# Down projection of a gated FFN as seven 128-token block products per 256 outputs, with a one-pass gate activation and VectorE's loop written out

## What is computed

```python
def conv_glu_ffn(h, w_up, conv_w, conv_b, w_down):
    u = causal_depthwise_conv(h @ w_up, conv_w) + conv_b
    gate, up = jnp.split(u, 2, axis=-1)
    return (jax.nn.gelu(gate, approximate=True) * up) @ w_down
...
        x = x + rms_norm(conv_glu_ffn(h, w_up[l], ffn_conv_w[l], ffn_conv_b[l], w_down[l]), ffn_post_norm[l])
```

## Time and profile before

| what | us |
|---|---|
| median of three runs | 1795.56 |
| lowest and highest of them | 1792.64, 1796.88 |
| span of the profiled execution, first to last instruction | 1791.1 |
| TensorE busy | 1704.2 |
| VectorE busy | 642.6 |
| ScalarE busy | 409.8 |

### The profile page before, as it was taken

How to read it: one execution, slowest core, us unless ns; L and a number is a source line. 1 busy time by engine, 2 the same in 40 slices (tenths; PEclk the granted TensorE clock), 3 DMA queues, 4 the chain that set the end, 5 groups by cost and what they waited for, 6 DMA issues and landing times.

```text
span 1791.1 us, 20952 instructions
## 1 busy us (share of the span) xinstructions
PE 1704.2 (95%) x8474; PEld 977.6 (55%) x8474; DVE 642.6 (36%) x1289; ACT 409.8 (23%) x797; POOL 32.2 (2%) x58
## 2 busy tenths in 40 slices
PE   9999999999999999999899999989899889988897
PEld 8778788887888888888623222322222222222232
DVE  3574466612759999941211101111010101111001
ACT  1143122201263544530111111111110111111112
POOL 4000000000000000100000000000000000000000
PEclk9999999999999999999999999999999999899999
DMA  5340244433453434276799999999999999999998
GB/s 187 118 188 13 83 157 148 163 148 116 166 191 118 168 133 169 104 291 249 304 374 433 433 425 436 430 430 433 431 430 430 430 431 435 430 432 428 432 432 335
DMA packets 36389, 523.07 MB, mean 292 GB/s; under 512 B 3880, under 2 KB 4072, under 8 KB 7784
## 3 DMA queue, kind: packets, MB, share of 16 engines
q1 hardware_dynamic: 35104, 511.75, 69.6%
q10 hardware_dynamic: 1224, 10.50, 1.6%
HBM read 521.12 MB, written 1.12 MB: 292 GB/s over the span
## 4 chain that ended last, share of the span: by engine, by line
PE 71%; DMA 24%; DVE 2%; SPq 1%; ACT 1%; another core or an unknown queue 1%; issue 0%; DVEq 0%; ACTq 0%
DMA arena<-in_experts 24%; PE psum L942 17%; PE psum L1282 13%; PE psum L593 12%; PE psum L1177 5%; PE psum L915 4%; PE psum L1026 3%; PE psum L1231 2%; PE psum L1007 1%; PE psum L1314 1%; PE psum L656 1%; PE psum L677 1%; PE psum L895 1%; PE psum L1201 1%; SPq L476 1%; PE psum L1296 1%
## 5 line engine op out<-in xcount | busy, mean ns | idle before, releaser
L1282 PE MATMUL psum<-arena 128*34 128x512 f32 x1792 | 409.1, 609 | 41.4 <-DMA arena<-in_experts 39.1
L2452 DVE SCALAR_TENSOR_TENSOR arena<-arena,psum 34x512 f32<-34x512 f32 x64 | 44.0, 687 | 758.2 <-ACT arena L1743 758.2
L942 PE MATMUL psum<-arena 128*128 128x272 f32 x1312 | 305.9, 392 | 0.0
L1282 PEld LDWEIGHTS psum<-arena 128*34 128x34 f32 x1792 | 106.2, 113 | 319.7 <-issue 272.9
L942 PEld LDWEIGHTS psum<-arena 128*128 128x128 f32 x1312 | 247.3, 189 | 53.1 <-issue 0.7
L1177 PE MATMUL psum<-arena 128*34 128x512 f32 x896 | 216.4, 639 | 9.8 <-DMA arena<-in_experts 9.8
L593 PE MATMUL psum<-arena 128*128 128x256 f32 x992 | 215.4, 378 | 0.0
L593 PEld LDWEIGHTS psum<-arena 128*128 128x128 f32 x992 | 187.3, 189 | 27.6 <-issue 1.2
L1177 PEld LDWEIGHTS psum<-arena 128*34 128x34 f32 x896 | 57.5, 118 | 157.7 <-issue 157.5
L1743 ACT ACTIVATE arena<-psum 34x512 f32<-34x512 f32 x64 | 37.9, 593 | 441.7 <-PE psum L1282 385.4
L2158 DVE SCALAR_TENSOR_TENSOR arena<-arena 128x272 f32<-128x272 f32 x240 | 111.0, 524 | 3.7
(11 more groups left out here) (444 smaller groups left out, 1367.2 us busy)
## 6 DMA issues: line engine op xcount, KB each, us to landing
arena<-in_experts SPq DMA_DIRECT2D x71, 4096.0 KB, 50.0
arena<-in_panels SPq DMA_DIRECT2D x91, 1024.0 KB, 4.8
arena<-in_experts SPq DMA_DIRECT2D x44, 2048.0 KB, 44.9
arena<-in_down_panels SPq DMA_DIRECT2D x8, 1408.0 KB, 5.9
arena<-in_experts SPq DMA_DIRECT2D x10, 1024.0 KB, 10.7
arena<-scr ACTq DMA_DIRECT2D x4, 2176.0 KB, 8.9
arena<-in_experts SPq DMA_DIRECT2D x4, 512.0 KB, 17.4
out<-arena SPq DMA_DIRECT2D x4, 256.0 KB, 2.1
```

The source lines that it names most:

```text
L942: ins = mm(pair[k][:, b, 0:T], slot8[k][:, c, b * P:(b + 1) * P], src[:, c, :], start=c == 0, stop=c == DC - 1)
L1282: ins = mm(psum[lo:lo + CAP, p % 2, :], xg[:, c, :], r_up[2 * p + x][:, c, :], start=c == 0, stop=c == DC - 1)
L2452: STT(es[gate_at, :], es[gate_at, :], 1.0, psum[gate_at, p % 2, :], ADD, MUL)
```

## The change

**Seven products.** Each group of 256 outputs is a product of a 2 x 2 block matrix (inputs in chunks of 128, even and odd; outputs in two halves of 128) with a 2 x 2 block matrix of `hid` (even and odd chunk; tokens 0 to 127 and 128 to 255). It is computed by seven block products in place of eight, with sums of weights (`S1` to `S4`) and of activations (`combined`, t1 to t4). Each of the seven runs over 11 blocks, so that there are 4 x 7 x 11 = 308 products of 128 x 128 weights and 128 columns. `w_down` comes as 16 quarters of 128 x 1408. The first eight are loaded beside the panels of the up projection, the third group's after the last panel, the fourth's after the first group is done (`second_done`).

**VectorE.** The 11 iterations are written out. Each also forms the four sums t1 to t4 of the iteration before (`combine`), and iterations 3 to 9 form one sum of weights of 1408 columns each (`down_sum`). The other nine sums of weights, the sums of the products (`keep`, `cross`) follow the loop. `hid_ready` is now raised by `combine`.

**ScalarE.** The four passes of the sigmoid become one hyperbolic tangent pass, with a table load ahead of the loop and one behind it. The last group's squares are taken in parts.

The diff, cut to what the steps below speak of:

```diff
-            panels(PANELS["w_up"] + 2, 20)
...
+            def quarter(i, q):
+                at = down_at[i] + QUARTER * q
+                sp.dma_start(unit(at), a["down_quarters"][i, q]).then_inc(ev(f"down{i}_loaded"), 16)
+            for j in range(10):
+                panel(PANELS["w_up"] + 2 + j)
+                if j > 1:
+                    quarter((j - 2) // 4, (j - 2) % 4)
+            panels(PANELS["w_up"] + 12, 10)
+            for last in (n[0] - 2, n[0] - 1):
+                sp.wait_ge(panel_done[last % 2], last // 2 + 1)
+            for q in range(4):
+                quarter(2, q)
+            sp.wait_ge(ev("second_done"), 1)
+            for q in range(4):
+                quarter(3, q)
...
-            for j in range(2):
-                pe.wait_ge(ev("hid_ready"), FB // 4 + 1 if j == 0 else FB // 2)
-                for i in range(4):
-                    k, m = n[0] % 2, n[0] // 2
-                    pe.wait_ge(slot_loaded[k], 16 * (m + 1))
-                    if j and i > 1:
-                        pe.wait_ge(copied[0], 20 + i - 1)
-                    for b in range(2):
-                        for c in range(11):
-                            ins = mm(down_at(i)[:, b, :], slot11[k][:, c, b * P:(b + 1) * P], hid[:, 11 * j + c, :],
-                                     start=j == 0 and i < 2 and c == 0, stop=j == 1 and c == 10, skip_group_check=True)
-                        if j == 1 and i == 3 and b == 0:
-                            ins.then_inc(ev("half_done"), 1)
-                    ins.then_inc(panel_done[k], 1)
-                    n[0] += 1
-            sum_added(pair[0][:, 0, :], 2, "ffn")
+            def product(into, weights, tokens, lo, hi, begins, ends):
+                w3 = weights.rearrange("p (m n) -> p m n", m=FB // 2)
+                for m in range(lo, hi):
+                    ins = mm(into, w3[:, m, :], tokens(m), start=begins and m == 0, stop=ends and m == FB // 2 - 1,
+                             skip_group_check=True)
+                return ins
+            def hidden(odd, x):
+                return lambda m: hid[:, 2 * m + odd, x * P:(x + 1) * P]
+            def combined(j):
+                return lambda m: raw_gate[:, 2 * (S + 2) * m + j * P:2 * (S + 2) * m + (j + 1) * P]
+            def first_product(i, lo, hi):
+                pe.wait_ge(ev(f"down{i}_loaded"), 64)
+                product(sum_11[i], A11[i], hidden(0, 0), lo, hi, True, False)
+            def first_products(i, lo, hi):
+                pe.wait_ge(ev("sums_ready"), 4 * i + 2)
+                product(sum_of(i, 2), S3[i], combined(2), lo, hi, True, False)
+                product(sum_of(i, 1), S1[i], combined(0), lo, hi, False, False)
+                pe.wait_ge(ev("sums_ready"), 4 * i + 3)
+                return product(sum_of(i, 0), S2[i], combined(1), lo, hi, False, True)
+            def second_products(i):
+                pe.wait_ge(ev("kept_ready"), i + 1)
+                pe.wait_ge(ev("sums_ready"), 4 * i + 4)
+                product(sum_of(i, 2), A22[i], combined(3), 0, FB // 2, False, True)
+                product(sum_of(i, 1), S4[i], hidden(1, 1), 0, FB // 2, False, True).then_inc(ev("cross_done"), 1)
+                return product(sum_11[i], A12[i], hidden(1, 0), 0, FB // 2, False, True)
+            early = FB // 2 - 1
+            pe.wait_ge(copied[1], n[0] // 2)
+            pe.wait_ge(ev("hid_ready"), early)
+            first_product(0, 0, early)
+            first_products(0, 0, early)
+            first_product(1, 0, early)
+            pe.wait_ge(ev("hid_ready"), FB // 2)
+            first_product(0, early, FB // 2)
+            first_products(0, early, FB // 2).then_inc(ev("first_done"), 1)
+            first_product(1, early, FB // 2)
+            first_products(1, 0, FB // 2).then_inc(ev("first_done"), 1)
+            second_products(0).then_inc(ev("second_done"), 1)
+            pe.wait_ge(copied[0], (n[0] + 1) // 2)
+            for i in (2, 3):
+                first_product(i, 0, FB // 2)
+                first_products(i, 0, FB // 2).then_inc(ev("first_done"), 1)
+                second_products(i - 1).then_inc(ev("second_done"), 1)
+            pe.nop().then_inc(slot_loaded[0], 64)
+            pe.nop().then_inc(slot_loaded[1], 64)
+            pe.wait_ge(ev("second_done"), 3)
+            pe.nop().then_inc(panel_done[0], 4)
+            pe.nop().then_inc(panel_done[1], 4)
+            second_products(3).then_inc(ev("second_done"), 1)
+            n[0] += 8
+            sum_added(pair[0][:, 0, :], 2, "ffn", 6)
...
+            nc.scalar.preload_act_table_set("exp_and_others")
             act.wait_ge(ev("gelu_in"), 1)
-            sigmoid(fe, fg, "gelu", 1).then_inc(ev("gelu_exp"), 1)
+            A(fe, fg, ACT.Tanh, scale=GELU_A * GELU_B / 2).then_inc(ev("gelu_exp"), 1)
...
-                sigmoid(fe, fg, "gelu", i + 1).then_inc(ev("gelu_exp"), 1)
+                A(fe, fg, ACT.Tanh, scale=GELU_A * GELU_B / 2).then_inc(ev("gelu_exp"), 1)
+            nc.scalar.preload_act_table_set("natural_log_exp_and_others")
...
+                else:
+                    act.wait_ge(ev("cross_ready"), 4)
+                    A(sq[:, 7, 0:S], fT[:, 7, :], ACT.Square).then_inc(ev("sq_ready"), 1)
+                    A(sq[:, 6, P:S], fT[:, 6, P:S], ACT.Square)
+                    act.drain()
+                    A(fT[:, 7, :], fT[:, 7, :], ACT.Copy, scale=gain(1))
+                    A(fT[:, 6, P:S], fT[:, 6, P:S], ACT.Copy, scale=gain(0))
+                    act.wait_ge(ev("second_done"), 4)
+                    A(sq[:, 6, 0:P], sum_11[3], ACT.Square).then_inc(ev("sq_ready"), 1)
+                    A(of_11, sum_11[3], ACT.Copy, scale=gain(0)).then_inc(copied[0], 4)
...
-            with dve.Fori(0, 11) as i:
+            def filtered(i):
...
-                TS(fg, fg, GELU_A * GELU_B, GELU_B, MUL, ADD)
-                dve.drain()
-                TT(fg, fg, gx, MUL).then_inc(ev("gelu_in"), 1)
-                sigmoid_arg(fe, fg, "gelu", i + 1)
+                STT(fg, fg, 1.0 / GELU_A, gx, ADD, MUL).then_inc(ev("gelu_in"), 1)
+            def gated(i):
                 dve.wait_ge(ev("gelu_exp"), i + 1)
-                TT(gx, fe, gx, MUL)
-                dve.drain()
-                TT(hid[:, bass.ds(i * 2, 2), :], gx, ux, MUL).then_inc(ev("hid_ready"), 1)
-                dve.drain()
-            add_squares("ffn", "sq_added")
+                STT(gx, fe, 1.0, gx, ADD, MUL)
+                dve.drain()
+                STT(hid[:, 2 * i:2 * i + 2, :], gx, 0.5, ux, MUL, MUL)
+                dve.drain()
+            def combine(i):
+                b11, b12, b21, b22 = [hid[:, 2 * i + odd, x * P:(x + 1) * P] for odd in range(2) for x in range(2)]
+                t1, t2, t3, t4 = [raw_gate[:, i * (2 * (S + 2)) + j * P:i * (2 * (S + 2)) + (j + 1) * P] for j in range(4)]
+                TT(t3, b22, b12, SUB)
+                TT(t1, b12, b11, SUB)
+                dve.drain()
+                TT(t2, t3, b11, ADD)
+                dve.drain()
+                TT(t4, b21, t2, SUB).then_inc(ev("hid_ready"), 1)
+            def down_sum(i, at):
+                dve.wait_ge(ev(f"down{i}_loaded"), 64)
+                dve.drain()
+                if at == 0:
+                    ins = TT(S1[i], S3[i], A22[i], ADD)
+                elif at == 1:
+                    ins = TT(S3[i], A11[i], S3[i], SUB)
+                elif at == 2:
+                    ins = TT(S2[i], S1[i], A11[i], SUB)
+                else:
+                    ins = TT(S4[i], A12[i], S2[i], SUB)
+                ins.then_inc(ev("sums_ready"), 1)
+            def keep(i):
+                p11, u2, u3 = [kept[i][:, at * P:(at + 1) * P] for at in range(3)]
+                dve.wait_ge(ev("first_done"), i + 1)
+                dve.drain()
+                CP(p11, sum_11[i])
+                dve.drain()
+                TT(u2, p11, sum_of(i, 0), ADD)
+                dve.drain()
+                TT(u3, u2, sum_of(i, 2), ADD)
+                dve.drain()
+                TT(fT[:, 2 * i + 1, P:S], u3, sum_of(i, 1), ADD).then_inc(ev("kept_ready"), 1)
+            def cross(i):
+                if i < 3:
+                    dve.wait_ge(ev("second_done"), i + 1)
+                else:
+                    dve.wait_ge(ev("cross_done"), 4)
+                u2 = kept[i][:, P:2 * P]
+                TT(fT_flat[:, 2 * i * S + P:2 * i * S + 3 * P].rearrange("p (a b) -> p a b", a=2),
+                   psum[:, 4 + i, P:3 * P].rearrange("p (a b) -> p a b", a=2), bcast(u2, 2, 1), ADD).then_inc(ev("cross_ready"), 1)
+            sums_in = {3: (0, 0), 4: (0, 1), 5: (0, 2), 6: (0, 3), 7: (1, 0), 8: (1, 1), 9: (1, 2)}
+            for i in range(11):
+                filtered(i)
+                if i:
+                    combine(i - 1)
+                if i in sums_in:
+                    down_sum(*sums_in[i])
+                gated(i)
+            combine(10)
+            keep(0)
+            down_sum(1, 3)
```

(36 more changed lines are left out.)

53 lines of the change are left out of this document (25 added, 28 removed).

## The result

The changed kernel is slower: 1803.97 us (1803.67 to 1805.51) against 1796.22 in the same series, a ratio of 1.0047 (95% interval 1.0033 to 1.0061), 7.75 us between the medians. In a second series, with 25 executions of the kernel before, it was 1802.92 against 1793.07, ratio 1.0059 (1.0039 to 1.0079). The forecast was slower by 4.3 us, 1799.9. The sign was right, the time lies inside the range, but the loss is about twice what was forecast.

What follows compares the result with a forecast made beforehand. TensorE was taken to bound the kernel, with DMA not full at the experts' border. Products -7.5, start +9.3, clock +1.7, waits +0.4, tail +0.4 gave +4.3 us: 1799.9 us, range 1796.3 to 1804.2.

Steps and rivals of the forecast that it cites:

- The products: Down projection on TensorE: 616 passes of 128 columns at 111.7 ns, 68.8 us against 76.26, a gain of 7.5 us.
- The rival of slower passes: Down projection: short passes wait for their weights, 121 ns each, +10.0 us, kernel 1805.6 us; chance 0.06.
- The start: Ahead of the down projection TensorE waits for the tenth `hid_ready`; first pass at 364.2 in place of 354.87, +9.3 us.
- The clock at the start: After the idle stretch ahead of the down projection the clock halves for about 3.4 us; +1.7 us, ends 0 and 3.4.
- the rival without it: Clock does not fall at the start, sum +2.6, 1798.2 us; chance 0.20 together with faster passes.
- The waits inside and the tail: Down projection: all waits but `second_done` 3 covered, +0.4 us; late last sums before L641's successor, +0.4 us.
- At nothing: VectorE's written iterations, ScalarE's table loads and tangent, and the early quarter loads run beside TensorE and cost nothing.
- What the FFN gains or loses before 431 us therefore reaches the end one for one: TensorE's chain runs without a hole to the experts, so no slack behind the FFN takes up its change.
- everything from L680 on shifted by the same amount: Sign to look for behind the down projection: all later work moves equally, and the shift arrives at the end.

Runs made afterwards that it cites:

- e_nine: Changed kernel with TensorE starting the down projection after nine block rows (45 products) in place of ten; 1793.61 us, ratio to before 0.9992.
- e_warm: Changed kernel with 19 unread matmuls of 256 columns in TensorE's wait ahead of the down projection; 1796.32 us, ratio to before 1.0016.
- e_vector: Kernel before with VectorE's iterations written out and the one-pass gate activation, old down projection, no sums; 1792.99 us, ratio to before 1.0005.
- s_before: Kernel before with four unread matmuls of 240 columns (1.6 us) between down projection and product sum; 1800.91 us, ratio to before 1.0036.
- after_again: The changed kernel, unchanged, run and profiled a second time; 1802.92 us, ratio to before 1.0059.
- e_nine_more: e_nine with the first nine block rows of the second group's other three products also ahead of the wait; 1788.25 us, ratio to before 0.9970.
- before_again: The kernel before, unchanged, run and profiled a second time; 1792.64 us, span 1789.5 us.
- s_after: Changed kernel with four unread matmuls of 240 columns (1.6 us) between down projection and product sum; 1799.69 us.

## Where the prediction was right, and why it was wrong

*The products.* 111.7 ns a pass were expected, 112 came. The 592 passes behind the first 5.5 us, with one gap of 0.45 us in them, behave as the 32 of L786 and L793. The rival of slower passes is out, and with it the rule of the Trainium skill ("TensorE: Matmul & The Clock Gate", "Back-to-back issue gap") as an estimate for this case: 97 us by it, 69 us by the passes.

*The start.* Expected +9.3, measured 8.7 in the same terms: 8.53 us of idle time, and 0.16 by which the first pass of L915 overlapped the end of L593. VectorE began 0.85 us behind the up projection's end (before: 1.05) and was through 7.58 us later, where the sum had 7.97; it ran the eight multiply-adds of the written loop in one piece of 3.42 us, without the gap of 0.20 that the earlier trace rows shows between them. The reason was right: TensorE goes on 0.10 us behind the tenth count, and in e_nine, where nine are asked for, the wait is gone.

*The clock at the start.* Expected +1.7 with ends of 0 and 3.4, measured 2.3 to 2.7 (26 passes at 213 ns are 2.6 more than at 111.7; 2.7 or 2.3 by e_warm). The idle stretch brought the fall, as the rule of the Trainium skill ("Why this matters for your kernels" on the same page) has it, and the rival without it is out.

*The waits inside and the tail.* The wait for `second_done` 3: 0.45 us idle, 0.6 with the restart, expected 0.4. All others were covered, as L933 is idle nowhere else in its 72.30 us: the sums of weights took 1.63 us (expected 1.61), the quarters landed 6.2 us after their issue. Of the tail's +0.4 at most 0.3 came: by the passes' spacing L665 could have started at 434.51; it started at 434.67, 0.05 behind VectorE's last add (L1884), and L667 0.97 behind it in place of 0.87. So the terms of the stage came out as -7.4, +8.7, +2.6, +0.6 and some +0.2, together the 4.7 measured: the wait was smaller, the clock's part larger than in the sum. The groups and the page's DMA row, answering to the earlier trace rows:

```profile
L2195 DVE TENSOR_TENSOR arena<-arena 128x1408 f32<-128x1408 f32 x4 | 6.5, 1626 | 0.4
```

```profile
arena<-in_down_quarters SPq DMA_DIRECT2D x16, 704.0 KB, 6.2
```

*At nothing.* e_vector bears it out: VectorE's and ScalarE's part without the sums costs and gives nothing that the runs can tell.

*The step that failed* is the first: "What the FFN gains or loses before 431 us therefore reaches the end one for one", and with it the sign "everything from L680 on shifted by the same amount". L680 stands 3.6 us later than L656 in the first profile of before, and the span ends 11.0 later. The stage's loss of 4.7 us did reach the end, but 7.4 us came on top in the profiles, 3 to 5 in the medians, which hold longer executions of before as well. The sum has a term for the clock at the start alone; behind the stage it stands at nothing, without a reason. I read the clock only where the change makes a new wait, and took the old waits as given, because their length does not change. The rows in hand spoke against that: of two waits of 2.5 us one was followed by a fall and one was not the earlier trace rows, so the trace of before showed that such a wait can go either way. What was missing from the sum is the price of the other way at each place: 0.7 us behind the wait before L680, 3.5 at the small products of `meta_rows`, 3.8 in the routing. Shifted by 1.6 us, the old stage pays it and the new one stops paying.

*What stays open:* what it is about a moment that brings the fall, and why all eight executions of the changed kernel are long (both that were profiled show the falls), where e_warm's and before's spread. That the time lies in the range, with 0.2 us to spare at the upper end, is luck: that end was set by terms of the stage, and the excess came from behind it.

## What to carry to other kernels

Start the consumer on what the producer finished an iteration earlier: one number in a wait (nine in place of ten) was worth 10 us of stage here (9.3 us between the medians of one series), more than the seven-product scheme itself (7.5). Dropping the eighth product pays only if the short passes still come at the rate of their columns, and if the blocks are ready before TensorE is. And where a difference below half a per cent is at stake, count the waits of one or two us, and the stretches of small products, on TensorE anywhere behind the change: a shift of 1.6 us alone switched the clock's falls on or off here, and with them as much time as the edit cost; shift the old kernel by a like amount before believing either sign.

## What the runs showed of the hardware

1.6 us of useless matmuls made one kernel 7.7 us slower and another about 3 us faster. The granted clock in the three windows was 1.00, 1.00, 0.93 or 0.89, 0.83, 0.86 for the same instructions behind the stage, and the part of the span that follows took 1360 or 1367 us. TensorE's work there is the same in both, and so is the wait of 2.55 us ahead of the first fall; what differs is the moment at which it comes. Behind that wait the clock fell where the next pass started at 430.09 (e_nine) or between 436.98 and 438.78 (s_before, e_warm, after_again, the changed kernel), and stayed up at 427.27 (e_nine_more), between 433.47 and 435.15 (e_vector, before_again, before) and at 440.03 (s_after). So later is not worse, and the time from the span's start isn't all of it: behind the wait of 1.09 us that ends at 153.65 in before and at 153.80 in before_again, in the same code, the 16 passes took 3.64 and 2.05 us. What about the moment decides is left open here.

A fall can follow a stretch with no wait at all: at `meta_rows` TensorE counts as busy throughout (20.00 of 20.00 us) in all profiles, on products of few columns in part, and the clock there (465 to 485) was 0.83 in the changed kernel's two profiles, in s_before's and in e_warm's, 0.84 in e_nine's, and 1.00 in five others.

Float32 passes of 128 columns with new weights for each come 112 ns apart over 592 of them, 256 columns 216.6 ns. Two passes of 128 columns (2 x 111.7) thus take 6.8 ns longer than one of 256, so the weight loads, one for each pass, are all but hidden, though their records last 189 to 192 ns (medians).
